# Eight input tiles accumulated side by side, k-outer, inside the modulation stage

## The chip, the cores and the metric

The kernel runs on one core of a Trainium2 chip, in one launch. The metric is the device time in microseconds. The core has TensorE (PE in the profile), whose weight loads have a row of their own (PEld), VectorE (DVE), ScalarE (ACT), GpSimd (POOL, here only an issuer of DMAs) and SyncE (SP, an issuer of DMAs). Each runs its own instruction list in order; semaphores tie them together.

## The reference, cut to what matters

Two layers of one block, then a second, different block that the change leaves alone.

```python
mod = silu(c) @ w_ada[l] + b_ada[l]
shift, scale, gate = jnp.split(mod, 3, axis=-1)
h = layernorm(x) * (1.0 + scale) + shift
p = h @ w_in[l]
u_f, z_f, cq, ckv, k_r, z_a = jnp.split(p, split_pts, axis=-1)
y_f = fourier_mix(u_f, w_fmix[l]) * silu(z_f)
q = rmsnorm(cq, q_norm[l]) @ w_q_b[l]
kv = rmsnorm(ckv, kv_norm[l]) @ w_kv_b[l]
y_a = attention(q, rope(q), kv, rope(k_r)) * silu(z_a)
y = jnp.concatenate([y_f, y_a], axis=-1) @ w_out[l]
x = layernorm(ALPHA * x + gate * y, ln_g[l], ln_b[l])
```

x has 256 tokens of 2048 channels. w_ada is 2048 x 6144 a layer, w_in 2048 x 3904. `fourier_mix` takes 8 groups of 128 channels, the real part of a two-dimensional Fourier transform over tokens and channels, and multiplies by a 128 x 128 matrix for each group.

## The kernel before, in words

Everything is float32 to full precision: each operand is cut into a high and a low part (`_hi`, `_lo`, ScalarE casts the high part, VectorE subtracts for the low one), and each product is three matmuls, `mm3` (L401): low weight by high activation, high by low, high by high.

**Weights** come as a stream of chunks of 128 x 2048 (1 MiB), loaded by SP into `raw`, which has three places. A chunk's `split` makes `w_hi` (ScalarE, L880) and `w_lo` (VectorE, L1266), each in two halves, into one of two slots. Chunk g + 2 is split once chunk g is used (`after`). `landed`, `hi_ready`, `lo_ready` and `weights_used` count along. In layer order the chunks are: seven tiles of 128 output columns (four of cq, two of ckv, one with k_r and its rotated copy), `L_DFT` (the matrix of the transform over tokens, split into `dft_hi`, `dft_lo`), `L_FMIX` (w_fmix and the channel transform), then u and z tiles alternately for eight groups, then heads and output. In one tile chunk all 16 row blocks k of the same 128 columns lie side by side, and PE makes 48 matmuls of 256 columns (`chunk`).

**Modulation.** For layer 0 shift and scale are computed first, from 32 chunks `ada0` of 1 MiB. Each is eight passes with csil (the silu of c) as a stationary operand of one column (`ada_row`, L539). The chunks have four places (three in `area`, one in `raw`); SP loads one when the chunk four before it is used. Four chunks make a row of 512 values, kept in PSUM bank 6 or 7. ScalarE copies it (`take_row`), PE turns it into columns (`turn_row`, L551), VectorE adds the bias (`read_mod0`). With two rows, a quarter of x (4 of 16 row blocks k) is normalised (`stage`), transposed by PE (`turn_tokens`, L453), scaled by ScalarE (`modulated`) and cut into `a_hi`, `a_lo` by VectorE (`split_modulated`). In layer 0 two tiles already run in quarters between the rows (`two_chunks`), from row 4 on; in layer 1 the same two run in quarters after the transposes (`first_two`).

All other modulation values (the gate of layer 0, all of layer 1 and its gate) are summed by VectorE: `add_ada` (L1283) multiplies a chunk of 128 x 2048 by one value a partition and adds it to `ada_acc`. GpSimd loads these chunks into a ring of two places, `ada_ring`, each when the add two before it is done. A layer makes 16 adds before its gate is summed by PE (`gate_sum`, L526). Seven of them stand in the seven-tile stretch, one behind each tile's split; then the groups make two each in groups 0 to 3, one in group 4, none in 5 and 6.

**After the seven tiles.** During each, ScalarE squares a tile (L951) and VectorE sums the squares for the rms norms. Then PE sums them over partitions (L590), waits for the DFT chunk, and makes the Fourier weight product: four `mm3` of 512 columns from `L_FMIX`, read by ScalarE (L962) and VectorE into `cw_hi`, `cw_lo`. Each group q is then: u tile into bank 0, `seq_dft(q-1)` into bank 2, z tile into bank 1, and the channel transform of u by `cw` into bank 3. ScalarE makes `u_hi`, `t_hi` (L988) and the tanh of z (L985), VectorE `u_lo`, `t_lo`, the gate product (`gate`) and y. `seq_dft(q)` waits for `t_lo` of group q. `latents` (L1497) makes the normalised cq and ckv out of PSUM after groups 4 and 5.

Of the kernel before, what the change touches and what calls it, by code (L numbers as in the profile page):

```python
# [21 lines left out]
ALU = mybir.AluOpType  # L22
# [3 lines left out]
P = 128  # L26
# [24 lines left out]
L_DFT = LAT  # L51
L_FMIX = LAT + 1
L_FOUR = LAT + 2
# [27 lines left out]
BLK = 512  # L81
R_GATE, R_LNG, R_LNB, R_MIX, R_MLP = 0, DEPTH, 2 * DEPTH, 3 * DEPTH, 3 * DEPTH + 1

# [25 lines left out]
def build(nc, stream, ada0, ada, vectors, rows, taps, consts, positions, x, meta, out):  # L109
    with ExitStack() as ctx:  # L110
# [93 lines left out]
        def ada0_slot(s):  # L204

            return raw[:, 2 * CH:3 * CH] if s == 3 else area[:, s * CH:(s + 1) * CH]

        def lat_ps(m):

            return bank(4 + m % 3, m // 3 * T)  # L210
# [37 lines left out]
        ada0_landed = [sem(f"ada0_landed{i}") for i in range(4)]  # L248
# [24 lines left out]
        cw_h, cw_l = sem("cw_h"), sem("cw_l")  # L273
# [35 lines left out]
        def _(sp):  # L309
            sp.dma_start(vec[:, :], vectors).then_inc(vec_in, 16)  # L310
            for s in range(4):
                sp.dma_start(ada0_slot(s), ada0[s]).then_inc(ada0_landed[s], 16)
# [6 lines left out]
            def load(g, par, waits):  # L319


                if waits:
# [7 lines left out]
            load(0, 0, False)  # L330
            load(1, 1, False)
            with sp.Fori(1, ADA0 // 4) as i:
                for s in range(4):
# [3 lines left out]
            sp.wait_ge(landed[0], 16)  # L337
            sp.wait_ge(ada0_used, ADA0)
            load(2, 0, False)
            sp.wait_ge(landed[1], 16)  # L340
            sp.wait_ge(lo_ready, 2)
            load(3, 1, False)
            with sp.Fori(2, CHUNKS // 2) as i:
# [56 lines left out]
        def _(pe):  # L400
            def mm3(o, w, a, first, last):  # L401

                pe.matmul(o, w[1], a[0], start=first, stop=False)  # L403
                pe.matmul(o, w[0], a[1], start=False, stop=False)  # L404
                return pe.matmul(o, w[0], a[0], start=False, stop=last)  # L405
# [29 lines left out]
            def turn_tokens(n, q):  # L435
# [18 lines left out]
                o.then_inc(tr_ps, 1)  # L454

# [75 lines left out]
            def ada_row(r):  # L531
                if r >= 2:
                    pe.wait_ge(row_in, r - 1)
                for s in range(4):
                    pe.wait_ge(ada0_landed[s], 16 * r + 16)
                    w = ada0_slot(s)
                    for k in range(4):
                        c = KT + 4 * s + k
                        o = pe.matmul(ps[32 * k:32 * k + 1, (6 + r % 2) * 512:(7 + r % 2) * 512], csil[:, c:c + 1],  # L539
                                      w[:, k * 512:(k + 1) * 512], start=s == 0, stop=s == 3)  # L540
                    o.then_inc(ada0_used, 1)

            def turn_row(r):
# [4 lines left out]
                if r >= 4:  # L548
                    pe.wait_ge(col_in, r // 2 - 1)
                for t in range(4):  # L550
                    o = pe.matmul(bank(2 + r // 2 % 2, 4 * (r % 2) + t, 1), row[:, t * P:(t + 1) * P],  # L551
# [5 lines left out]
            for r in range(ADA0 // 4):  # L557
                ada_row(r)
                if r:
                    turn_row(r - 1)  # L560
                if r == 1:
# [3 lines left out]
                if r == 2:  # L565
                    pe.wait_ge(ln_var, NORM["meta"] + 1)
                    turn_tokens(0, 0)
                if r in (4, 6):
                    turn_tokens(0, r // 2 - 1)
                    two_chunks(0, (lat_ps(0), lat_ps(1)), a_ops, 0, r // 2 - 2)  # L570
            turn_tokens(0, 3)
            turn_row(ADA0 // 4 - 1)
            two_chunks(0, (lat_ps(0), lat_ps(1)), a_ops, 0, 2)
            two_chunks(0, (lat_ps(0), lat_ps(1)), a_ops, 0, 3)

            for l in range(DEPTH):
                G = l * PER_LAYER

                if l:
                    first_two(G, (lat_ps(0), lat_ps(1)), a_ops, 1)  # L580
                for m in range(2, LAT - 1):
                    if m >= 3:
                        pe.wait_ge(lat_sq, 6 * l + m - 2)
                    chunk(G + m, (G + m) % 2, lat_ps(m), a_ops)
                if l:
                    pe.wait_ge(mod_ready, 3)
                chunk(G + LAT - 1, (G + LAT - 1) % 2, bank(7), a_ops)

                pe.wait_ge(lat_acc, 6 * (l + 1))
                pe.matmul(bank(3, 0, 2 * T), ones[:, :], sc[:, 0:2 * T], start=True, stop=True)\  # L590
                    .then_inc(lat_stat, 1)

                pe.wait_ge(lo_ready, 2 * (G + L_DFT) + 2)
                pe.wait_ge(weights_used, G + L_DFT)
                pe.nop().then_inc(weights_used, 1)
# [4 lines left out]
                pe.wait_ge(kr_rot, l + 1)  # L600
                for j, b in enumerate((0, 1, 2, 7)):
                    o = mm3(bank(b, 0, 512), wb(g % 2, 8 + j // 2), wb(g % 2, 4 * (j % 2), 512), True, True)
                o.then_inc(weights_used, 1)

                def seq_dft(q, first):

                    pe.wait_ge(t_l, 8 * l + q + 1)
                    if first:
                        pe.wait_ge(cw_l, 4 * l + 3)
# [9 lines left out]
                def group(q, first, second=False):  # L619
                    g = G + L_FOUR + 2 * q  # L620
                    g0 = G + L_FOUR
                    if first:
                        pe.wait_ge(cw_l, 4 * l + 1)
                    chunk(g, g0 % 2, bank(0), a_ops)
                    if first:
                        pe.wait_ge(cw_l, 4 * l + 2)
                    else:
                        seq_dft(q - 1, second)
                        pe.wait_ge(z_ready, 16 * l + q)
                    chunk(g + 1, (g0 + 1) % 2, bank(1), a_ops)  # L630
                    pe.wait_ge(u_l, 8 * l + q + 1)
                    if first:
                        pe.wait_ge(cw_l, 4 * (l + 1))
                        pe.wait_ge(ln_var, NORM[f"lat{l}"] + 1)
                    for j in range(2):
                        o = mm3(bank(3, j * T), (u_hi[:, j * P:(j + 1) * P], u_lo[:, j * P:(j + 1) * P]),
                                (cw_hi[:, bass.ds(q * T, T)], cw_lo[:, bass.ds(q * T, T)]), True, True)
                    o.then_inc(t_ps, 1)

                group(0, True)  # L640
                group(1, False, True)
                with pe.Fori(2, GROUPS - 1) as q:
                    group(q, False)
                gate_sum(l)
                group(GROUPS - 1, False)
# [6 lines left out]
                def project(h, first):  # L652

                    g = G + L_HEAD + 2 * h
                    par = (G + L_HEAD) % 2
# [1435 lines left out]
```

## Time and profile before

| what | us |
|---|---|
| median of 3 runs | 2208.07 |
| lowest, highest run | 2205.77, 2210.68 |
| profiled execution, its own time | 2209.09 |
| its span, first to last instruction | 2207.3 |
| PE busy | 2044.4 |
| weight loads busy | 1879.5 |
| VectorE busy | 1446.1 |
| ScalarE busy | 911.8 |
| granted clock of TensorE, mean share of full speed | 0.958 |

The span is that of one profiled execution, and its instruction times add up to it, not to the median. Busy shares are means over stages with different limits, so a stage has to be read by itself. In a timeline a row is start, duration, engine, line, operation, what it writes and reads, count; a bracket gives the idle time before it and what ended it. Matmuls overlap, so their distance is the cost of one, not their duration. A stored count x8 on L539 is one chunk. Times of the trace are us from the span's start.

### The profile page before, as it was taken

Reading aid. Unit: us, or ns where it says so; the run is one execution under the profiler, and the core shown is the slowest. Engines: PE = TensorE matmul, PEld = TensorE weight load, DVE = VectorE, ACT = ScalarE, POOL = GpSimd, SP = SyncE. Lnnn points to the kernel's source line nnn. Section 1 sums busy time; section 2 is a strip of 40 time slices with the busy share of each in tenths; the row PEclk is TensorE's granted clock in tenths of the full one; section 3 lists DMA queues with packets and bytes.
Section 4 is the critical chain, followed back from the end, with each engine's and each line's share of the span. In section 5 each row is a group of like instructions: output and inputs, shape, how many; then the busy total and the mean of one; then the engine's idle time right before and its main releaser. Section 6 shows DMA issues by size and latency. Waiting matters only on the chain.

```text
span 2207.3 us, 37641 instructions
## 1 busy us (share of the span) xinstructions
PE 2044.4 (93%) x14132; PEld 1879.5 (85%) x14132; DVE 1446.1 (66%) x1923; ACT 911.8 (41%) x1347; POOL 39.0 (2%) x77
## 2 busy tenths in 40 slices
PE   4889997985899999699997999989999999999998
PEld 1489997875899998599997999879989989989986
DVE  3288787798786665788898545555555545545545
ACT  2143454432344553343334334445434434434443
POOL 0000000000000000000000000000000000000000
PEclk7799998996999999899998999999999999999999
DMA  9898577593884445244453554544555555555553
GB/s 389 360 364 310 200 272 265 224 344 135 310 326 148 153 164 193 103 172 172 175 186 119 186 186 178 189 170 171 190 191 184 185 197 182 185 193 188 189 190 134
DMA packets 64192, 462.08 MB, mean 209 GB/s; under 512 B 7120, under 2 KB 7632, under 8 KB 8176
## 3 DMA queue, kind: packets, MB, share of 16 engines
q1 hardware_dynamic: 53696, 385.33, 47.4%
q0 software_dynamic: 10416, 75.63, 9.3%
q8 instruction: 57, 0.93, 0.2%
q14 instruction: 23, 0.19, 0.0%
HBM read 458.83 MB, written 2.10 MB: 209 GB/s over the span
## 4 chain that ended last, share of the span: by engine, by line
PE 78%; DVE 11%; DMA 6%; issue 3%; ACT 2%; DVEq 0%; SPq 0%; ACTq 0%; POOLq 0%
PE ps L403 25%; PE ps L404 25%; PE ps L405 25%; DVE w_lo L1266 3%; DMA raw<-in_ada 3%; DMA area<-in_ada 3%; DVE area L1288 2%; ACT w_hi L880 1%; PE ps L539 1%; DVE X L1649 0%; PE ps L453 0%; ACT sc L1036 0%; DVE X L1643 0%; DVE st L1274 0%; PE ps L516 0%
## 5 line engine op out<-in xcount | busy, mean ns | idle before, releaser
L1266 DVE TENSOR_TENSOR w_lo<-raw,w_hi 128x1024 fp32r<-128x1024 f32 x658 | 777.3, 1221 | 347.3 <-ACT w_hi L880 345.6
L403 PE MATMUL ps<-a_hi,w_lo 128*128 128x256 f32 (+1 forms) x2912 | 829.4, 285 | 16.9 <-DVE y_lo L1274 7.2
L880 ACT CAST w_hi<-raw 128x1024 fp32r (+1 forms) x658 | 656.3, 1047 | 439.7 <-PE ps L405 430.6
L404 PE MATMUL ps<-a_lo,w_hi 128*128 128x256 f32 (+1 forms) x2912 | 827.8, 284 | 0.0
L405 PE MATMUL ps<-a_hi,w_hi 128*128 128x256 f32 (+1 forms) x2912 | 826.6, 284 | 0.0
L403 PEld LDWEIGHTS ps<-a_hi,w_lo 128*128 128x128 f32 x2912 | 556.1, 191 | 20.5 <-DVE y_lo L1274 8.1
L405 PEld LDWEIGHTS ps<-a_hi,w_hi 128*128 128x128 f32 x2912 | 556.1, 191 | 0.0
L404 PEld LDWEIGHTS ps<-a_lo,w_hi 128*128 128x128 f32 x2912 | 553.1, 190 | 0.7 <-issue 0.5
L403 PE MATMUL ps<-w_hi,y_lo 128*128 128x512 f32 x768 | 300.4, 391 | 6.1 <-DVE w_lo L1266 6.1
L404 PE MATMUL ps<-w_lo,y_hi 128*128 128x512 f32 x768 | 299.4, 390 | 0.0
L405 PE MATMUL ps<-w_hi,y_hi 128*128 128x512 f32 x768 | 299.3, 390 | 0.0
L403 PEld LDWEIGHTS ps<-w_hi,y_lo 128*128 128x128 f32 x768 | 144.6, 188 | 38.1 <-DVE w_lo L1266 8.2
L405 PEld LDWEIGHTS ps<-w_hi,y_hi 128*128 128x128 f32 x768 | 144.5, 188 | 30.3
L404 PEld LDWEIGHTS ps<-w_lo,y_hi 128*128 128x128 f32 x768 | 144.6, 188 | 29.4
L1288 DVE SCALAR_TENSOR_TENSOR area<-area,csil 128x2048 f32<-128x2048 f32 x64 | 150.3, 2349 | 20.2 <-DMA area<-in_ada 17.2
L1205 ACT ACTIVATE sc<-ps 128x256 f32<-128x256 f32 x64 | 24.6, 385 | 180.6 <-PE ps L405 180.6
L1900 DVE TENSOR_TENSOR sc<-sc 128x256 f32<-128x256 f32 x64 | 27.3, 426 | 105.2 <-ACT sc L1205 105.2
L403 PE MATMUL ps<-y_hi,w_lo 128*128 128x256 f32 x272 | 78.7, 289 | 8.9 <-DVE y_lo L1816 5.8
L404 PE MATMUL ps<-y_lo,w_hi 128*128 128x256 f32 x272 | 78.4, 288 | 0.0
L405 PE MATMUL ps<-y_hi,w_hi 128*128 128x256 f32 x272 | 78.3, 288 | 0.0
L1274 DVE TENSOR_TENSOR st<-ps,st 128x256 fp32r<-128x256 f32 (+1 forms) x98 | 48.0, 505 | 20.6 <-ACT st L980 17.8
L403 PEld LDWEIGHTS ps<-y_hi,w_lo 128*128 128x128 f32 x272 | 53.6, 197 | 9.2 <-issue 6.0
(229 smaller groups left out, 1935.7 us busy)
## 6 DMA issues: line engine op xcount, KB each, us to landing
raw<-in_stream SPq DMA_DIRECT2D x331, 1024.0 KB, 4.8
area<-in_ada POOLq DMA_DIRECT2D x64, 1024.0 KB, 5.3
area<-in_ada SPq DMA_DIRECT2D x24, 1024.0 KB, 8.0
raw<-in_ada SPq DMA_DIRECT2D x8, 1024.0 KB, 9.3
grow<-in_rows POOLq DMA_DIRECT2D x4, 1024.0 KB, 5.1
area<-in_rows POOLq DMA_DIRECT2D x4, 1024.0 KB, 7.1
X<-in_x SPq DMA_DIRECT2D x1, 2048.0 KB, 15.2
out<-X SPq DMA_DIRECT2D x4, 512.0 KB, 2.6
```

The lines of the kernel that those rows point to most:

```text
L403: pe.matmul(o, w[1], a[0], start=first, stop=False)
L404: pe.matmul(o, w[0], a[1], start=False, stop=False)
L405: return pe.matmul(o, w[0], a[0], start=False, stop=last)
L539: o = pe.matmul(ps[32 * k:32 * k + 1, (6 + r % 2) * 512:(7 + r % 2) * 512], csil[:, c:c + 1], w[:, k * 512:(k + 1) * 512], start=s == 0, s ...
L880: ac.copy(to, raw[:, bass.ds((g % RAW) * CH + h * n, n)]).then_inc(hi_ready, 1)
L1205: ac.activation(sc[:, b * T:(b + 1) * T], bank(b), ACT.Relu).then_inc(f_relu, 1)
L1266: ve.tensor_tensor(to, raw[:, bass.ds((g % RAW) * CH + h * n, n)], hi.bitcast(F32), ALU.subtract).then_inc(lo_ready, 1)
L1274: return ve.tensor_tensor(out_, exact, hi.bitcast(F32), ALU.subtract)
L1288: ve.scalar_tensor_tensor(out=ada_acc, in0=ada_ring[:, par * CH:(par + 1) * CH], scalar=csil[:, bass.ds(KT + a % KT, 1)], in1=ada_acc, op0 ...
L1900: ve.tensor_tensor(s, r, r, ALU.mult).then_inc(f_sq, 1)
```

## The change

The first eight column tiles of a layer (the seven, and u of group 0) are stored in two column blocks of four tiles; a chunk now holds four row blocks k of four tiles (`by_block`), and there are eight such chunks in the order quarter, column block (`FIRST = 8`). PE works through them in `piece`s: one row block k, four tiles, 12 matmuls. All eight tiles stay open in PSUM banks 4 to 7, two tiles a bank.

In layer 0 a piece stands behind each modulation chunk from number 10 on, 22 in all, and the last ten follow. The stream's eight chunks are loaded between modulation chunks 4 and 31. The modulation chunks have three places, not four, and the row stays in one bank. In layer 1 the eight chunks run as four quarters (`quarter_of`) between the transposes.

Then the Fourier weight product comes at once (`L_FMIX` before `L_DFT`), z of group 0 into bank 2 with the norm's sum in the middle of it, and the channel transform of u. Squares and their sums are made after the eight tiles. `slot_of` gives the slot of a chunk, now that the DFT chunk uses none. Of the 16 adds of a layer, three stand ahead of group 0, two in each of groups 0 to 5 and one in group 6.

```diff
-L_DFT = LAT
-L_FMIX = LAT + 1
-L_FOUR = LAT + 2
+FIRST = 8
+L_FMIX = FIRST
+L_DFT = FIRST + 1
+L_FOUR = FIRST + 1
...
-            return bank(4 + m % 3, m // 3 * T)
+            return bank(4 + m // 2, m % 2 * T)
...
-            with sp.Fori(1, ADA0 // 4) as i:
-                for s in range(4):
-                    sp.wait_ge(ada0_used, 4 * i + s - 3)
-                    sp.dma_start(ada0_slot(s), ada0[bass.ds(4 * i + s, 1)].rearrange("a p n -> (a p) n"))\
-                        .then_inc(ada0_landed[s], 16)
...
+            for c in range(3, ADA0):
+                sp.wait_ge(ada0_used, c - 2)
+                sp.dma_start(ada0_slot(c % 3), ada0[c]).then_inc(ada0_landed[c % 3], 16)
+                if c % 8 in (4, 6):
+                    g = c // 8 * 2 + (c % 8) // 6
+                    load(g, g % 2, g >= 2)
+            with sp.Fori(FIRST // 2, CHUNKS // 2) as i:
...
+            def piece(l, q, j, kk):
+
+                g, k = l * PER_LAYER + 2 * q + j, 4 * q + kk
+                if kk % 2 == 0:
+                    half(g, kk // 2)
+                    pe.wait_ge(ln_lo, 8 * l + k // 2 + 1)
+                for m in range(4):
+                    at = j * CH + kk * BLK + m * P
+                    o = mm3(lat_ps(4 * j + m), (w_hi[:, at:at + P], w_lo[:, at:at + P]), a_ops(k),
+                            k == 0 and m % 2 == 0, k == KT - 1, True)
+                if kk == 3:
+                    o.then_inc(weights_used, 1)
...
+            for c in range(ADA0):
+                ada_chunk(c)
+                if c % 4 == 0 and c:
+                    turn_row(c // 4 - 1)
...
+                if c % 8 == 7:
+                    turn_tokens(0, c // 8)
+                if c >= 10:
+                    n = c - 10
+                    if n == 0:
+                        pe.wait_ge(ln_var, NORM["meta"] + 1)
+                    piece(0, n // 8, n % 8 // 4, n % 4)
+            piece(0, 2, 1, 2)
             turn_row(ADA0 // 4 - 1)
+            piece(0, 2, 1, 3)
+            quarter_of(0, 3)
...
+                    turn_tokens(1, 0)
+                    turn_tokens(1, 1)
+                    quarter_of(1, 0)
+                    for q in range(1, 4):
+                        if q < 3:
+                            turn_tokens(1, q + 1)
+                        quarter_of(1, q)
...
+                g = G + L_FOUR + 1
+                pe.wait_ge(cw_l, 4 * l + 2)
+                half(g, 0)
+                blocks(slot_of(g), bank(2), a_ops, range(8), True, False)
+                pe.wait_ge(lat_acc, 6 * (l + 1))
+                pe.wait_ge(cw_l, 4 * l + 4)
+                pe.matmul(bank(1, 0, 2 * T), ones[:, :], sc[:, 0:2 * T], start=True, stop=True)\
+                    .then_inc(lat_stat, 1)
+                half(g, 1)
+                blocks(slot_of(g), bank(2), a_ops, range(8, 16), False, True).then_inc(weights_used, 1)
...
@@ VectorE, a layer from its eighth tile on
-                    add_ada(A + m, (A + m) % 2)
+                lat_add(0)
+                lat_add(1)
                 cw(0)
                 cw(1)
-                after(G + L_FMIX, G + L_FMIX)
+                split(G + L_DFT, None, True)
+                split(G + L_DFT + 1, 1)
                 cw(2)
                 cw(3)
+                for m in range(2, QT + CT):
+                    lat_add(m)
+                split(G + L_DFT + 2, 0)
+                ve.wait_ge(lat_stat, l + 1)
...
                 def group(q, first, adds=2, late=False):
-                    a0 = A + (2 if late else LAT)
+                    a0 = A + 3 if not late else A + 2
...
+                    gate(q, 2 if first else 1)
+                    if first:
+                        add_ada(a, a0 % 2)
                     after_ada(g + 1, g0 + 1, a + 1, (a0 + 1) % 2, adds > 1)
                     ve.wait_ge(t_h, 8 * l + q + 1)
                     sub_hi(t_lo, bank(3, 0, 2 * T), t_hi).then_inc(t_l, 1)
 
+                for a in range(3):
+                    add_ada(A + a, a % 2)
                 group(0, True)
                 with ve.Fori(1, GROUPS // 2) as q:
                     group(q, False)
-                group(GROUPS // 2, False, 1)
+                group(GROUPS // 2, False)
                 latents(range(3))
-                group(GROUPS // 2 + 1, False, 0)
+                group(GROUPS // 2 + 1, False)
                 latents(range(3, QT + CT))
-                group(GROUPS // 2 + 2, False, 0)
+                group(GROUPS // 2 + 2, False, 1)
```

## Rows read from the trace of the kernel before

**Rows 1.** Windows: PE, PEld, DVE, ACT, POOL busy us (xcount), granted clock, DMA share, GB/s

```profile
5.00:105.40 100.40, 65.04 (x402) 24.75 (x403) 27.21 (x59) 17.97 (x30) 1.19 (x2) 0.75 0.93 381
105.40:142.90 37.50, 36.24 (x289) 36.04 (x290) 31.05 (x31) 14.59 (x22) 3.18 (x6) 0.94 1.00 394
142.90:180.90 38.00, 32.11 (x228) 30.01 (x227) 30.39 (x30) 18.76 (x24) 2.65 (x5) 0.91 0.85 321
534.30:579.90 45.60, 44.32 (x353) 44.09 (x354) 35.99 (x42) 17.01 (x28) 3.18 (x6) 0.94 0.65 242
579.90:620.30 40.40, 32.63 (x228) 30.63 (x227) 30.57 (x30) 17.46 (x23) 2.65 (x5) 0.87 0.79 303
620.30:692.20 71.90, 71.90 (x586) 69.98 (x586) 59.17 (x68) 32.08 (x50) 3.18 (x6) 1.00 0.70 255
```

**Rows 2.** Timeline of PE, modulation stage: start us, us, what, idle before

```profile
27.18 1.89 PE L539 MATMUL ps<-area,csil 128*1 128x512 f32 x8 [12.01 <-DMA area<-in_ada]
29.67 1.71 PE L539 MATMUL ps<-area,csil 128*1 128x512 f32 x8 [0.60 <-DMA area<-in_ada]
...
62.64 1.89 PE L539 MATMUL ps<-area,csil 128*1 128x512 f32 x8 [1.35 <-DMA area<-in_ada]
...
69.06 1.05 PE L551 MATMUL ps<-csil,rs 128*128 128x1 f32 x8
69.97 1.07 PE L453 MATMUL ps<-con,grow 128*128 128x128 f32 x8
...
100.52 1.04 PE L539 MATMUL ps<-raw,csil 128*1 128x512 f32 x8 [1.88 <-DMA raw<-in_ada]
...
103.84 1.70 PE L551 MATMUL ps<-csil,rs 128*128 128x1 f32 x8
```

**Rows 3.** Timeline of PE: matmuls at either clock

```profile
71.12 0.28 PE L405 MATMUL ps<-a_hi,w_hi 128*128 128x256 f32 x1
...
105.77 0.41 PE L404 MATMUL ps<-a_lo,w_hi 128*128 128x256 f32 x1
105.98 0.41 PE L405 MATMUL ps<-a_hi,w_hi 128*128 128x256 f32 x1
```

**Rows 4.** Timeline of PE, layer 1, after a wait

```profile
593.16 0.58 PE L403 MATMUL ps<-a_hi,w_lo 128*128 128x256 f32 x1 [4.45 <-DVE y_lo L1274]
```

**Rows 5.** Timeline of DVE, layer 0

```profile
107.36 0.69 DVE L1274 TENSOR_TENSOR a_lo<-grow,a_hi 128x512 fp32r<-128x512 f32 x1
...
149.13 2.35 DVE L1288 SCALAR_TENSOR_TENSOR area<-area,csil 128x2048 f32<-128x2048 f32 x1 [2.20 <-DMA area<-in_ada]
151.40 2.35 DVE L1266 TENSOR_TENSOR w_lo<-raw,w_hi 128x1024 fp32r<-128x1024 f32 x2
153.67 1.28 DVE L1274 TENSOR_TENSOR y_lo<-ps,y_hi 128x512 fp32r<-128x512 f32 x2
...
158.34 0.87 DVE L1495 TENSOR_SCALAR rs<-ps 128x256 f32<-128x256 f32 x2
...
172.68 0.68 DVE L1274 TENSOR_TENSOR st<-ps,st 128x512 fp32r<-128x512 f32 x1
```

**Rows 6.** Timeline of ACT, layer 0

```profile
126.08 0.39 ACT L951 ACTIVATE sc<-ps 128x256 f32<-128x256 f32 x1 [3.41 <-PE ps L405]
126.36 1.99 ACT L880 CAST w_hi<-raw 128x1024 fp32r<-128x1024 f32 x2
131.76 0.39 ACT L951 ACTIVATE sc<-ps 128x256 f32<-128x256 f32 x1 [3.41 <-PE ps L405]
...
151.65 1.07 ACT L962 CAST y_hi<-ps 128x512 fp32r<-128x512 f32 x2 [4.58 <-PE ps L405]
```

**Rows 7.** DMA issues, 583 to 660 us: KB each, median us to landing

```profile
area<-in_ada POOLq DMA_DIRECT2D x8, 1024.0 KB, 5.1
```

**Rows 8.** Timeline of DVE, layer 1, around the latents

```profile
665.26 3.34 DVE L1501 RECIPROCAL rs<-rs 128x512 f32<-128x512 f32 x1
...
671.36 0.42 DVE L1274 TENSOR_TENSOR st<-ps,st 128x256 fp32r<-128x256 f32 x1
```

More of the change, by code:

```diff
@@ L247, in build @@
         weights_used = sem("weights_used")
-        ada0_landed = [sem(f"ada0_landed{i}") for i in range(4)]
+        ada0_landed = [sem(f"ada0_landed{i}") for i in range(3)]
         ada0_used = sem("ada0_used")
@@ L319, in load @@
             def load(g, par, waits):
-                if waits:
+                if waits and isinstance(g, int):
+                    if g >= RAW:
+                        sp.wait_ge(lo_ready, 2 * g - 2 * RAW + 2)
+                    sp.wait_ge(landed[par], 8 * (g - par))
+                elif waits:
                     split_before = sp.snap(sp.to_reg(2 * g - 2 * RAW + 2))
@@ L400, in _, with mm3 @@
         def _(pe):
[L401 to L405, printed above, removed]
+            def mm3(o, w, a, first, last, shared=False):
+                pe.matmul(o, w[1], a[0], start=first, stop=False, skip_group_check=shared)
+                pe.matmul(o, w[0], a[1], start=False, stop=False, skip_group_check=shared)
+                return pe.matmul(o, w[0], a[0], start=False, stop=last, skip_group_check=shared)
             def wb(par, k, n=P):
@@ L454, in turn_tokens, with quarter_of @@
                 o.then_inc(tr_ps, 1)
+            def piece(l, q, j, kk):
[9 more added lines that the diff above has]
+                    o.then_inc(weights_used, 1)
+            def quarter_of(l, q):
+                for p in range(8):
+                    piece(l, q, p // 4, p % 4)
             def two_chunks(g, outs, ops, n, q):
@@ L528, in gate_sum, with ada_chunk @@
                 o.then_inc(ada_summed, 1)
[L531 to L541, printed above, removed]
+            def ada_chunk(c):
+                r, s = divmod(c, 4)
+                if r and s == 0:
+                    pe.wait_ge(row_in, r)
+                pe.wait_ge(ada0_landed[c % 3], 16 * (c // 3 + 1))
+                for k in range(4):
+                    at = KT + 4 * s + k
+                    o = pe.matmul(ps[32 * k:32 * k + 1, 2 * 512:3 * 512], csil[:, at:at + 1],
+                                  ada0_slot(c % 3)[:, k * 512:(k + 1) * 512], start=s == 0, stop=s == 3)
+                o.then_inc(ada0_used, 1)
             def turn_row(r):
@@ L617, in seq_dft, with group @@
                     o.then_inc(yf_ps, 1)
-                def group(q, first, second=False):
+                def group(q, second=False):
                     g = G + L_FOUR + 2 * q
[L621 to L633, printed above, removed]
-                        pe.wait_ge(ln_var, NORM[f"lat{l}"] + 1)
[L635 to L641, printed above, removed]
+                    g0 = slot_of(G + L_FOUR + 2)
+                    chunk(g, g0, bank(0), a_ops)
+                    seq_dft(q - 1, second)
+                    if second:
+                        pe.wait_ge(ln_var, NORM[f"lat{l}"] + 1)
+                    pe.wait_ge(z_ready, 16 * l + q)
+                    chunk(g + 1, 1 - g0, bank(1), a_ops)
+                    to_tokens(q)
+                group(1, True)
                 with pe.Fori(2, GROUPS - 1) as q:
-                    group(q, False)
+                    group(q)
                 gate_sum(l)
-                group(GROUPS - 1, False)
+                group(GROUPS - 1)
                 pe.wait_ge(lat_l, 6 * (l + 1))
@@ L1062, in _ @@
                     root("pre1b", 1, 1e-6)
-                    ac.wait_ge(mod_ready, 3)
-                    for q in range(4):
-                        modulated(1, q)
                 else:
@@ L1254, in _, with split @@
             own = Chain(ve, dve)
-            def split(g, par, dft=False, halves=range(2)):
+            def split(g, slot, dft=False, halves=range(2)):
                 n = HALF // 2 if dft else HALF
@@ L1448, in _ @@
             stage(0, 0)
+            stage(0, 1)
             for q in range(4):
+                split(2 * q, 0)
                 read_mod0(q)
@@ L1452, in _ @@
                 split_modulated(0, 2 * q + 1)
-                if q < 3:
-                    stage(0, q + 1)
-            ve.wait_ge(ada0_used, ADA0)
+                split(2 * q + 1, 1)
+                if q < 2:
+                    ve.wait_ge(ln_lo, 2 * q + 2)
+                    stage(0, q + 2)
             clear_ada(2)
@@ L1700, in _ @@
                             stage(1, q + 2)
+                        if q:
+                            for j in range(2):
+                                split(PER_LAYER + 2 * q + j, j)
                 else:
```

223 lines of the change are left out of this document (105 added, 118 removed).

## The prediction

> **What bounds the kernel now.** The page's table of 40 slices showed where PE is not full: near the start, briefly at each layer's latent stage, and at the end of each layer. Windows cut at the events the change touches [rows 1], and the timelines of PE, DVE and ACT, were read next. In the modulation stage (5 to 105.4 us) the DMA engines are 93% busy and PE's busy time contains long waits: this stage is paid by transfers. From 105.4 PE streams products with a DVE that is itself 80 to 85% busy in the seven-tile stretch. From 142.9 to 180.9 (last latent-type tile, to the end of the second z tile) and from 579.9 to 620.3 PE has idle time and a lower granted clock; afterwards it is full until 692.2. So three bounds follow one another: DMA, then PE, then for a few microseconds the chain ACT, DVE, PE around the Fourier product.
>
> **The modulation stage after the change.** Thirty-two modulation chunks and two stream chunks are loaded under it now, and eight stream chunks later: six more. Neighbouring chunks land 2.49 us apart [rows 2], so six cost 15 us of transfer, less the some 7 us in 5 to 105.4 in which DMA was not busy. The serial order by 2.49 us puts modulation chunk 10 at 42 us. That is the first with a `piece` behind it.
>
> The 48 matmuls of a tile take 5.68 us (squares at 126.08 and 131.76 [rows 6]), 0.118 each. A piece is 12 of them: 1.42 us or, at the lower clock with one every 0.21 us, 2.56 us [rows 3]. A chunk's own eight passes take 1.04 or 1.89 us (0.97 without the overlapping tail), a turned row 1.05, a turned quarter 1.07 [rows 2]. Eight chunks thus ask 8 x (0.97 + 1.42) + 1.07 + 2 x 1.05, or 22.3 us of PE at the higher clock, against 10 transfers or 24.9 us. It fits, but not evenly: no stream load comes between chunks 7 and 12, PE falls up to 3 us behind there, and with three slots, not four, that delays the next load. Following the order by hand gives 25.6 us for each eight and 113.7 us for the last landing; saturated DMA would give 109. A drop of the granted clock at the gap beside a stream load (the chunk behind a 1.35 us wait took 1.89 [rows 2]) costs 1 to 3 us more. I take 115, bounds 109 and 123.
>
> Behind the last chunk: its passes, transposes, three pieces and a turned row, 5.9 us to the row's end; 2.5 us until the first low halves (103.84 + 1.70 to 107.36 + 0.69 in the row of two [rows 2, 5]); then eight pieces, 11.4 us, and 0.7 us for a slow start: 20.5. Eight tiles are finished at Q = 135.5. Before, seven were at 142.9 and u0 needed 48 x 0.118 = 5.7 more. Up to Q, layer 0 gains 13 us.
>
> **Layer 1 up to Q.** PE starts at 534.3 as before. Eight tiles are 384 x 0.118 = 45.4 us, two quarters of transposes 2.1, the low clock at the start 2.4: Q = 584.2, against 579.9 for seven. The two weight splits a quarter need 4 us of ACT and 4.7 of DVE [rows 5, 6] beside 11.4 us of PE and are hidden. The old waits between the quarters of two tiles (a little over 1 us) go.
>
> **From Q to the second z tile.** Here the change moves work the wrong way. The seven `add_ada` that DVE made in the tile stretch, in time that it had, now stand behind the squares, splits and Fourier products: three before `group(0)`, two in it, all ahead of the `t_lo` for which PE's first `seq_dft` waits, in front of all later PE work.
>
> DVE after Q: u_lo and kr 0.5 to 1.3 us; two squares in turn with ACT (0.39 and 0.42 each) to 2.6; two Fourier low halves of 0.64 to 3.9; the DFT split 1.3 (half the columns of a 2.35 one) to 5.2; the z0 split 2.35 to 7.5; two more low halves to 8.8; four squares in turn with ACT to 11.9; the split of u1, whose ACT half is free only at 12.45, to 14.8; the sums 0.87, to 15.7 [rows 5, 6]. PE starts z0 at 6.5, waits for the squares in the middle of it, and ends u1 near 22.
>
> Then the adds, 2.35 each [rows 5]: two landed long ago, to 20.4. The ring has two places, so the third load is issued when the first add ends (18.05) and lands 5.1 us after its issue [rows 7], which comes 0.7 us behind the add (0.53 of it GpSimd's own, 3.18 us for six [rows 1]): 23.9, add to 26.2. gate 26.6. The fourth has landed, to 29.0. The fifth's load leaves at 26.2, lands 32.0, add to 34.4. Split of the next chunk 36.7, t_lo 37.3. PE has stood for 15 us, from Q+22.2. Then seq_dft 1.4, z1 5.7, and 1.6 us because matmuls after a wait run at the lower clock (0.58 us behind a 4.45 us wait [rows 4], 20 of them at 0.213 in place of 0.118): z1 ends at Q + 46.0.
>
> The Trainium skill, "DMA: Bandwidth & Descriptors", section "Anatomy of one DMA", gives a fixed 2.0 us plus bytes by 436 GB/s for a load issued by GpSimd, an estimate of 4.4 us for 1 MiB, where the row has 5.1. By the page each of the two waits would be 0.7 us shorter and z1 would end at Q + 44.6; the row decides.
>
> Layer 0: 135.5 + 46.0 = 181.5 against 180.9, +0.6. Layer 1: 584.2 + 46.0 = 630.2 against 620.3, +9.9. Bounds of the 46.0: 39.5 if no add waited for its load, 49 if the loads meet the stream's.
>
> **Groups 4 to 6.** Before, these made one add; now five, 9.4 us more, next to the latents (reciprocal 3.34, latents of three tiles until 671.36 [rows 8]). DVE in 620.3 to 692.2 is 59.17 of 71.9 us busy [rows 1], and much of the rest is waiting for ACT inside a group. Laid over the old timeline: group 4's extra add makes the split for u6 late by 2.3 us, group 5's two make t_lo late by another 2.4. Together +4.7 per layer, bounds 0 (the gaps take it all) and 8. Groups 1 to 3 keep their two adds. Heads, output and the second block keep their work. The moved PSUM banks and the weight slot indices cost nothing: same instructions, and each reader is still ahead of the next writer.
>
> **Sum.** +0.6 + 9.9 + 2 x 4.7 = +19.9 us. The profiled execution took 2209.09 us with a span of 2207.3, so 2229.0 on its scale; the median shown is 1.0 lower: 2228. A coarser check is by DVE work alone: at Q in layer 1 it owes six adds more than at 579.9 (14.1 us) and starts 4.3 us later; of its 22 idle us until 692.2 it may win back 3 to 10. That gives +8 to +15, mine is +14.6.
>
> **Rivals.** (A) The forecast, chance 0.58, own range 2217 to 2239.
>
> (B) Faster: the 13 us gained up to Q in layer 0 stand because t_lo comes in time. With PE never waiting for t_lo, z1 ends at Q + 30.9: -14.5 in layer 0, -5.2 in layer 1, and with the group losses 2198. Each us of PE's wait for the first t_lo costs 2 us (two layers); the sign turns at 5 us of wait, I have 15. For it: DVE has idle time before Q. Against: adds are in program order behind it. Chance 0.14.
>
> (C) Slower still: TensorE's granted clock falls in the modulation stage. Eight chunks then ask 41 us of PE, not 22.3. With half of them at the lower clock, 9.5 us per eight less 3.3 us of slack, over 21 chunks: +16 us, 2244. For it: 62 to 69 us ran slow with short waits. Against: when PE is behind it has no gaps. Chance 0.13. The Trainium skill, "TensorE: Matmul & The Clock Gate", section "HAM oscillation", describes this: products of a tile shorter than the wait for its next slice, so that each tile starts slow. By it every stream gap would begin slow and (C) would be the likelier; the rows show both outcomes in this stage.
>
> (D) The lower bounds together: DMA saturated (-6), group losses absorbed (-9.4), t_lo 3 us earlier in each layer (-6): 2207. Chance 0.15, of which 0.09 within the band.
>
> **Numbers.** 0.2% (4.4 us) is what a measurement of this kernel tells from no change. Slower: A, C and 0.06 of D, 0.77; same 0.09; faster 0.14. The range from 2204 to 2243 leaves out B and half of C.
>
> **What the new profile would show.** The chunks after number 10 about 3.2 us apart on average and the last matmul of the modulation near 115; two rows of pieces at 0.28, not 0.41; the first Fourier product near 136 and 584; a PE wait of 10 to 18 us ended by DVE's `t_lo` in each layer, with two DVE waits on `area<-in_ada` before it; short PE waits on `w_lo` or `t_lo` in groups 5 and 6. Wrong if this wait is under 5 us, or if pieces in the modulation stage are mostly 0.41.

## The result, and the profile after

The kernel before took 2206.96 us (median of 4 runs, 2205.77 to 2210.68), the changed one 2231.68 us (median of 4, 2226.5 to 2233.33). The ratio is 1.0105, with a 95% interval of 1.0084 to 1.0126: slower by 24.7 us. The forecast was 2228, with a range of 2204 to 2243. The profiled execution of the changed kernel is its fastest: 2226.5 us with a span of 2224.8, which is 17.5 more than the span before. All ratios are of fast runs alone: one run of experiment 1, slow at 4033 us, is left out.

**Windows of the changed kernel**, cut at the same events as those of before, with two more inside the modulation stage. The columns are those of [rows 1].

```profile
20.00:40.00 20.00, 10.60 (x50) 2.00 (x50) 8.07 (x23) 5.53 (x9) 0.00 (x0) 0.59 1.02 424
65.00:120.00 55.00, 46.99 (x368) 30.69 (x368) 15.11 (x22) 14.22 (x20) 0.00 (x0) 1.00 0.98 385
120.40:140.30 19.90, 18.77 (x157) 17.73 (x158) 8.77 (x11) 6.40 (x9) 1.72 (x3) 1.00 0.79 287
140.30:186.10 45.80, 26.86 (x178) 25.17 (x178) 32.40 (x35) 17.88 (x28) 3.16 (x6) 0.78 0.67 252
538.60:587.60 49.00, 48.97 (x401) 49.00 (x402) 25.61 (x32) 18.13 (x24) 0.53 (x1) 0.96 0.46 165
587.60:633.20 45.60, 26.77 (x178) 25.07 (x178) 32.39 (x35) 16.57 (x27) 3.17 (x6) 0.81 0.69 258
633.20:709.60 76.40, 72.75 (x590) 70.42 (x589) 67.28 (x72) 31.96 (x50) 5.28 (x10) 1.00 0.78 282
```

The gain is in the second and third lines: PE works through the pieces at full granted clock under the loads, and the eight tiles are done at 140.3. Before, the seven were done at 142.9. The loss is in the two lines of 46 us. Each of them holds the work from the eighth tile to the second z tile. PE is busy for less than 27 of 46 us, while before it was busy for 32 of 38 and 33 of 40 [rows 1].

**PE waits by releaser, changed kernel**: first from 105 to 300 us (layer 0), then from 545 to 740 us (layer 1). The columns are the total in us, the number of waits and the longest.

```profile
PE ps L408 <- DVE st L1315: 17.0, 2, 15.0
PE ps L408 <- DVE w_lo L1307: 5.1, 2, 3.4
...
PE ps L408 <- DVE st L1315: 16.9, 2, 14.9
PE ps L408 <- DVE w_lo L1307: 5.1, 2, 3.4
```

L1315 on `st` is here the low half `t_lo`. One wait of 15 us a layer stands for the first of them, and one of 2.0 us for a later one. The split `w_lo` adds 3.4 and 1.7 us.

**Timeline of PE, changed kernel, layer 0**: the transposes of the first quarter of x, a matmul of a piece, the last modulation chunk, and the two waits.

```profile
41.46 1.97 PE L458 MATMUL ps<-con,grow 128*128 128x128 f32 x8 [4.39 <-DVE grow L1385]
...
71.03 0.28 PE L410 MATMUL ps<-a_hi,w_hi 128*128 128x256 f32 x1
...
120.41 1.04 PE L562 MATMUL ps<-area,csil 128*1 128x512 f32 x8 [2.21 <-DMA area<-in_ada]
...
146.44 0.35 PE L408 MATMUL ps<-a_hi,w_lo 128*128 128x256 f32 x1 [3.42 <-DVE w_lo L1307]
...
176.88 0.58 PE L408 MATMUL ps<-st 128*128 128x256 f32 x1 [15.04 <-DVE st L1315]
```

**Timeline of DVE, changed kernel, layer 0**, while PE stands.

```profile
151.97 2.36 DVE L1307 TENSOR_TENSOR w_lo<-raw,w_hi 128x1024 fp32r<-128x1024 f32 x2 [0.51 <-ACT w_hi L908]
154.24 0.88 DVE L1541 TENSOR_SCALAR rs<-ps 128x256 f32<-128x256 f32 x2
155.03 4.81 DVE L1329 SCALAR_TENSOR_TENSOR area<-area,csil 128x2048 f32<-128x2048 f32 x2
163.54 2.35 DVE L1329 SCALAR_TENSOR_TENSOR area<-area,csil 128x2048 f32<-128x2048 f32 x1 [3.70 <-DMA area<-in_ada]
165.81 0.41 DVE L1578 SCALAR_TENSOR_TENSOR zs<-th,ps 128x256 f32<-128x256 f32 x1
166.14 2.35 DVE L1329 SCALAR_TENSOR_TENSOR area<-area,csil 128x2048 f32<-128x2048 f32 x1
171.61 2.35 DVE L1329 SCALAR_TENSOR_TENSOR area<-area,csil 128x2048 f32<-128x2048 f32 x1 [3.12 <-DMA area<-in_ada]
173.88 2.35 DVE L1307 TENSOR_TENSOR w_lo<-raw,w_hi 128x1024 fp32r<-128x1024 f32 x2
176.15 1.01 DVE L1315 TENSOR_TENSOR st<-ps,st 128x512 fp32r<-128x512 f32 x2
```

This is the forecast's chain: five adds of 2.35 us (the row x2 holds two) and two waits for a load, 3.70 and 3.12 us, all between the norm sums and the `t_lo` that releases PE. In layer 1 the same two waits are 3.24 and 3.49 us. The loads behind them, GpSimd's from 583 to 660 us, beside those of [rows 7]:

```profile
area<-in_ada POOLq DMA_DIRECT2D x10, 1024.0 KB, 5.3
```

**Timeline of DVE, the gate sum's end in each layer**: first the kernel before, then the changed one.

```profile
252.90 2.47 DVE L1314 TENSOR_TENSOR grow<-grow,ps 128x512 f32<-128x512 f32 x4
...
692.30 2.47 DVE L1314 TENSOR_TENSOR grow<-grow,ps 128x512 f32<-128x512 f32 x4
```

```profile
263.00 2.47 DVE L1355 TENSOR_TENSOR grow<-grow,ps 128x512 f32<-128x512 f32 x4
...
710.16 2.47 DVE L1355 TENSOR_TENSOR grow<-grow,ps 128x512 f32<-128x512 f32 x4
```

The first `a_lo` of layer 1 is at 533.5 before and 537.8 after. So the account of the 17.5 us of span is: layer 0 up to its gate +10.1; heads and output, up to that `a_lo`, 274.8 us against 280.6, or -5.8; layer 1 up to its gate 172.4 against 158.8, or +13.6; the rest -0.4. The change leaves the code of that stretch alone, and other kernels with the same code there take 276.5 to 278.9 us (last section), so at least a part of the -5.8 is chance of this one execution. Without it the sum is +23.3, near the 24.7 of the medians.

### The profile page after: what moved, and what is told of

It is laid out like the page before. It is cut to its first block, busy times and chain, and to the rows that moved or that the text cites. A ratio compares the mean times of both kernels' runs of the same rounds, so it can differ in the third digit from the quotient of the medians.

```text
span 2224.8 us, 37536 instructions
## 1 busy us (share of the span) xinstructions
PE 2035.9 (92%) x14132; PEld 1875.1 (84%) x14132; DVE 1445.0 (65%) x1923; ACT 911.7 (41%) x1347; POOL 38.9 (2%) x77
## 4 chain that ended last, share of the span: by engine, by line
PE 76%; DVE 13%; DMA 5%; issue 3%; ACT 2%; DVEq 0%; ACTq 0%; POOLq 0%; SPq 0%
PE ps L408 24%; PE ps L409 24%; PE ps L410 24%; DMA area<-in_ada 5%; DVE w_lo L1307 4%; DVE area L1329 2%; PE ps L562 1%; ACT w_hi L908 1%; DVE st L1315 1%; PE ps L458 1%; DVE X L1699 0%; DVE y_lo L1315 0%; ACT sc L1080 0%; DVE X L1693 0%; PE ps L539 0%
## 5 line engine op out<-in xcount | busy, mean ns | idle before, releaser
L408 PEld LDWEIGHTS ps<-a_hi,w_lo 128*128 128x128 f32 x2912 | 555.3, 191 | 36.2 <-issue 27.7
L408 PE MATMUL ps<-st 128*128 128x256 f32 x160 | 47.8, 299 | 40.3 <-DVE st L1315 40.3
L562 PE MATMUL ps<-area,csil 128*1 128x512 f32 x256 | 38.8, 686 | 33.9 <-DMA area<-in_ada 33.2
```

The costliest lines, as they stand in the source:

```text
L408: pe.matmul(o, w[1], a[0], start=first, stop=False, skip_group_check=shared)
L562: o = pe.matmul(ps[32 * k:32 * k + 1, 2 * 512:3 * 512], csil[:, at:at + 1], ada0_slot(c % 3)[:, k * 512:(k + 1) * 512], start=s == 0, stop ...
```

## The experiments

The theory going in: DVE's adds, moved behind the eighth tile, cost the time, and the loads of a ring of two places lengthen them. Its rivals: other parts of the new order, or a modulation stage in which PE is late. Ratios are to the kernel before, run beside the changed one on the same chip. Medians of different experiments come from different chips, so they compare less well than ratios.

**1. Both adds of group 0 behind `t_lo`.**

```diff
+                    after_ada(g + 1, g0 + 1, a + 1, (a0 + 1) % 2, adds > 1 and not first)
+                    ve.wait_ge(t_h, 8 * l + q + 1)
+                    sub_hi(t_lo, bank(3, 0, 2 * T), t_hi).then_inc(t_l, 1)
                     if first:
                         add_ada(a, a0 % 2)
-                    after_ada(g + 1, g0 + 1, a + 1, (a0 + 1) % 2, adds > 1)
-                    ve.wait_ge(t_h, 8 * l + q + 1)
-                    sub_hi(t_lo, bank(3, 0, 2 * T), t_hi).then_inc(t_l, 1)
+                        add_ada(a + 1, (a0 + 1) % 2)
```

> Changed kernel, with the two adds of group 0 behind t_lo instead of ahead of it. Adds theory: t_lo of group 0 ends 7 to 8 us earlier in each layer (two adds of 2.35 us and one wait of 3.1 to 3.5 us for a load), PE's wait of 15.0 us for it falls to about 7.5, and the time from 2231.7 to about 2217. Rival (the new order around the Fourier product, with its squares and splits, sets the wait, and the adds only fill it): the wait stays at 13 to 15 us and the time within 3 us of 2231.7.

Measured: 2228.02 us, ratio 1.0107 (1.0084 to 1.0131), no change that the times can tell, where about 2217 was expected. The PE waits of layer 0 (105 to 300 us) in this kernel:

```profile
PE ps L408 <- DVE st L1315: 11.1, 3, 6.9
PE ps L408 <- DVE w_lo L1307: 6.4, 3, 3.4
```

The first wait fell from 15.0 to 6.9 us as expected, but others came back behind it, and the gate was only 3.1 us earlier in either layer. The forecast of this run took the wait for the cost. What costs is what DVE owes: two adds and their loads, put behind one `t_lo`, delay the next one.

**2. The five adds ahead of the first `t_lo` on 16 of their 2048 columns.** The rest of these terms is left out of the modulation sums.

```diff
-            def add_ada(a, par):
+            def add_ada(a, par, n=CH):
...
-                    add_ada(A + a, a % 2)
+                    add_ada(A + a, a % 2, 16)
```

> Changed kernel; the five adds of each layer that stand ahead of the first t_lo take only 16 of their 2048 columns (the other columns of these five terms are left out), semaphores and loads as before. It parts DVE's time in them from the waits for their loads. Adds theory: 11 us of DVE time go, but the loads still come two at a time with about 5.8 us from add to landing, so t_lo ends 6 to 7 us earlier in each layer and two waits on area<-in_ada are longer than before; time near 2218. Were the waits for loads nothing, it would be 11 us a layer and 2210. Rival (adds only fill a wait that others set): no change of the wait for t_lo, 2231.

Measured, in a single run: 2218.94 us beside 2203.86 for the kernel before, so 15.1 more than it, against 24.7 for the whole change. The gate of layer 0 comes 5.0 us earlier than in the changed kernel, and layer 1 is 4.7 us shorter up to its gate. The timeline of DVE in layer 0:

```profile
162.17 0.23 DVE L1329 SCALAR_TENSOR_TENSOR area<-area,csil 128x16 f32<-128x16 f32 x1 [6.79 <-DMA area<-in_ada]
165.60 0.24 DVE L1329 SCALAR_TENSOR_TENSOR area<-area,csil 128x16 f32<-128x16 f32 x1 [2.87 <-DMA area<-in_ada]
168.08 0.23 DVE L1329 SCALAR_TENSOR_TENSOR area<-area,csil 128x16 f32<-128x16 f32 x1 [2.24 <-DMA area<-in_ada]
170.50 1.01 DVE L1315 TENSOR_TENSOR st<-ps,st 128x512 fp32r<-128x512 f32 x2
```

With the arithmetic nearly gone, `t_lo` comes 5.6 us earlier, not 11: the loads of the ring set the pace instead. PE's wait is still 9.6 us.

**3. One product in place of three in the 22 pieces of layer 0's modulation stage.** The two low products of these pieces are left out.

```diff
-                    piece(0, n // 8, n % 8 // 4, n % 4)
+                    piece(0, n // 8, n % 8 // 4, n % 4, True)
```

> Changed kernel; the 22 pieces between the modulation chunks make one product in place of three (low parts left out, only there). It asks why the last modulation chunk came at 120.4 us and not at the 109 of an unbroken DMA. Theory (with three places PE's lateness delays the next load): the last chunk's passes begin at 109 to 112 us, and the time is 8 to 10 us less, near 2222. Rival (the transfers themselves are slower than 2.49 us each): they begin at 118 or later and the time falls by less than 3 us.

Measured, in a single run: 2231.42 us, and the last chunk's passes begin at 120.19 (120.41 in the changed kernel). So it is not PE's products that delay the last landing. This kernel's windows:

```profile
40.00:65.00 25.00, 19.81 (x100) 8.63 (x100) 12.34 (x20) 7.58 (x11) 0.00 (x0) 0.93 0.78 314
65.00:120.00 55.00, 38.88 (x240) 18.35 (x240) 14.93 (x22) 14.19 (x20) 0.00 (x0) 0.82 0.98 396
```

With a third of the product work the DMA engines still idle a fifth of 40 to 65 us and then move 396 GB/s. The idle part lies in one place. The changed kernel, and then that of experiment 7:

```profile
40.00:46.00 6.00, 4.54 (x28) 2.75 (x32) 4.63 (x10) 1.32 (x2) 0.00 (x0) 0.63 0.34 109
46.00:65.00 19.00, 14.65 (x116) 8.89 (x108) 7.83 (x12) 6.41 (x9) 0.00 (x0) 1.00 0.99 404
...
40.00:46.00 6.00, 6.00 (x31) 2.41 (x33) 2.39 (x6) 1.55 (x4) 0.00 (x0) 0.50 0.71 247
```

Behind modulation chunk 7 PE waits 4.39 us for DVE to normalise the first quarter of x (the 41.46 row above). The next chunk is used only afterwards, so no place comes free, SP's queue waits up to 7.5 us for these passes, and the DMA engines run dry: 34% busy in 40 to 46 us, 99% from there to 65. With one product this wait is 4.40 us and the share 25%. So PE does hold the loads back once, by a wait and not by its work.

**4. The kernel before, with nothing but the adds' new places**: `add_ada` taken out of the seven-tile stretch, three ahead of group 0, two in each of groups 0 to 5 and one in group 6.

```diff
-                    add_ada(A + m, (A + m) % 2)
...
+                for a in range(3):
+                    add_ada(A + a, a % 2)
```

> The kernel before, tiles and Fourier product as they were; only VectorE's adds are placed as in the changed kernel: none in the seven tiles, three ahead of group 0, two in groups 0 to 5, one in group 6. Adds theory: t_lo of group 0 comes 6 to 8 us too late for PE, groups 4 to 6 lose 4 to 5 us, in each layer: 2207 becomes 2227 to 2233. Rival (the adds cost nothing where they stand, the tiles' new order costs): within 4 us of 2207.

Measured: a median of 2223.95 us, 20.1 more than the kernel before (2203.86), the low end of the 20 to 26 that were expected; the ratio is 1.0105 (1.0066 to 1.0143), that of the whole change. One of the four runs took 2237.17 us, 13 more than the next, and widens the interval; the two medians alone make 1.0091. The PE waits of layer 0:

```profile
PE ps L403 <- DVE w_lo L1266: 7.5, 4, 2.8
PE ps L403 <- DVE st L1274: 6.1, 2, 4.1
```

No single wait here is longer than 4.1 us, yet the gate of layer 0 comes 7.7 us later than before (260.61), and layer 1 takes 8.4 us more from its first `a_lo` to its gate (707.87 less 540.65, against 158.8). Moved alone, in the old order of everything else, the adds cost two thirds of the change's 23.7 us by stage (10.1 and 13.6) and by the ratio as much as all of it, with an interval from 15 to 32 us. So most of the loss needs no other part of the change.

**5. In layer 1, six adds in the quarters, one ahead of group 0**, then 2, 2, 2, 2, 1, 0, 0 in the groups. GpSimd loads four chunks more ahead of the gate row.

```diff
+                                add_ada(5 * KT + 2 * (q - 1) + j, j)
...
-                for a in range(3):
+                for a in (range(6, 7) if l else range(3)):
...
-                group(GROUPS // 2, False)
+                group(GROUPS // 2, False, 1 if l else 2)
```

> Changed kernel; in layer 1 alone six adds stand behind the weight splits of quarters 1 to 3, one ahead of group 0, and the groups have 2, 2, 2, 2, 1, 0 and 0 as in the kernel before; GpSimd loads four of these chunks ahead of the gate's row. Debt theory (it is DVE's total of adds behind the eighth tile that counts, not where they stand in it): six adds are paid in idle time, PE's wait for the first t_lo of layer 1 falls from 15 us to about 4, the waits of groups 5 and 6 of layer 1 go; 15 us less than the changed kernel, ratio to the kernel before near 1.004. Rival (the Fourier part sets the wait): less than 4 us off, ratio 1.009 or more.

Measured: ratio 1.0062 (1.0047 to 1.0078), clearly below the changed kernel's but short of the 1.004 expected. Layer 1 from its first `a_lo` to its gate takes 160.3 us, 12.1 less than 172.4, where 15 was expected. PE's wait for the first `t_lo` fell to 6.4 us, not to 4, and the waits of groups 5 and 6 are gone. One of the two load waits is left:

```profile
617.04 2.35 DVE L1333 SCALAR_TENSOR_TENSOR area<-area,csil 128x2048 f32<-128x2048 f32 x1 [2.80 <-DMA area<-in_ada]
```

**6. Four of a layer's adds in groups 4 to 6 on 16 columns**, the rest of these terms left out.

```diff
...
-                group(GROUPS // 2 + 1, False)
+                group(GROUPS // 2 + 1, False, n=(16, 16))
...
```

> Changed kernel; the second add of group 4 and those of groups 5 and 6 (four a layer) take only 16 of 2048 columns (the rest of these terms is left out). Theory: PE's waits of groups 5 and 6 go, 4 to 5 us a layer, 8 to 10 us in all: ratio to the kernel before near 1.0065. Rival (these adds stand in gaps, the forecast's lower bound): within 2 us of the changed kernel, ratio 1.010.

Measured: the two later waits are gone, and the stages are 4.8 us (layer 0) and 4.4 us (layer 1) shorter, as the forecast's +4.7 a layer asks. The ratio, 1.0094 (1.0078 to 1.0109), moved by only 0.0011, less than its interval can tell; the expected 1.0065 lies outside the interval, the rival's 1.010 inside. In the profiled execution the span is only 3.8 us shorter, though the two stages are 9.2 us shorter: the stretch between layer 0's gate and layer 1 took 3.7 us more. So the profile bears out the two waits and their price by stage, and the times do not show that the whole kernel gains them.

**7. The stream's loads spread evenly over the modulation stage**, one behind every fourth chunk, the eighth behind the last.

```diff
-                if c % 8 in (4, 6):
-                    g = c // 8 * 2 + (c % 8) // 6
+                if c % 4 == 0:
+                    g = c // 4 - 1
                     load(g, g % 2, g >= 2)
+            load(7, 1, True)
```

> Changed kernel; the stream loads of the modulation stage come one behind every fourth modulation chunk (4, 8, ... 28) and the eighth behind the last, in place of two close together in each eight. Theory of the order (PE falls behind in the long stretch without stream load): the last modulation chunk's passes begin 3 to 5 us earlier, near 116, and the kernel is as much faster: ratio near 1.009. Rival, which the run with one product speaks for (transfers run at some 385 GB/s in this stage whatever PE does): only the one transfer moved behind the last chunk shows, 2.5 us, ratio 1.0095 or more.

Measured: ratio 1.0082 (1.0063 to 1.0101). The last chunk's passes begin at 114.09, 6.3 us earlier, and the gate of layer 0 comes 6.9 us earlier. Windows of this kernel:

```profile
40.00:65.00 25.00, 24.58 (x171) 13.60 (x169) 9.62 (x14) 7.00 (x10) 0.00 (x0) 0.85 0.91 360
65.00:120.00 55.00, 48.56 (x387) 33.02 (x384) 15.35 (x24) 14.23 (x20) 1.19 (x2) 1.00 0.98 399
```

The DMA engines are 91% busy in 40 to 65 us, where the changed kernel has 83%, and move 360 GB/s against 334. The order of the loads is worth about 6 us of layer 0, and it is a cost of its own beside the adds. An estimate of its parts: 2.5 us is the one stream load that now follows the last chunk, and 2.0 us the DMA idle time that the hole at 40 to 46 us no longer has (17% of 25 us less 9%); the rest is the higher rate behind it. It is not the long stretch without a stream load that is mended, as the theory had it: one stream load instead of two now stands ahead of chunk 7, so PE's wait for x ends at 38.56 us and not at 41.46, while the DMA engines still have the other one to move. The ratio alone does not part theory and rival: 1.009 and 1.0095 both lie inside its interval.

**8. All of it**: the edits of 5 and 7; in layer 0 the first two adds behind the split of the last modulated quarter and one ahead of group 0; in both layers the second add of group 0 behind `t_lo`. Then **9, the same without the edit of 7**.

```diff
-            clear_ada(2)
+            add_ada(ADA0, 0)
+            add_ada(ADA0 + 1, 1)
...
-                for a in range(3):
+                for a in (range(6, 7) if l else range(2, 3)):
```

> Changed kernel with layer 1's adds early (as in e3), the loads spread (as in e6), and in layer 0: ada_acc cleared as soon as the last modulation chunk is used, adds 0 and 1 behind the split of chunk 7, one add ahead of group 0, and in both layers the second add of group 0 behind t_lo. Debt theory: 15 us from layer 1, about 9 from layer 0 (two adds and both waits for loads leave the path to t_lo), 2.5 to 4 from the loads: ratio to the kernel before 0.996 to 1.000. Rival (the order of adds is worth little): ratio above 1.004.

> The kernel of e7_all without its spreading of the loads: the changed kernel with the adds of both layers placed as in e7_all, the stream's loads in the changed kernel's order. If the two costs are separate, as e6_loads_spread put them (the loads' order 6.3 us of layer 0's last modulation chunk, the adds the rest), the last chunk's passes begin at 120 us, not 114, and the time lies 6 to 7 us above e7_all's, 2203 where the kernel before has 2206, a ratio of 0.998 to 1.000. If the early loads are what lets the adds come early in layer 0, the waits for the first t_lo come back in part there as well and the time is 2207 or more, a ratio above 1.000.

Measured for all of it: 2196.35 us, ratio 0.9957 (0.9943 to 0.9970), better than both kernels. Without the spread loads: 2203.21 us, ratio 0.9989 (0.9976 to 1.0002), no longer to be told from the kernel before; the last chunk's passes begin at 121.53, and no wait for `t_lo` is longer than 2.0 us. The PE waits of the first of the two, in layer 0 and then in layer 1:

```profile
PE ps L413 <- DVE st L1320: 6.0, 4, 2.0
PE ps L413 <- DVE w_lo L1312: 5.1, 2, 3.4
...
PE ps L413 <- DVE w_lo L1312: 3.4, 1, 3.4
PE ps L413 <- DVE st L1320: 3.0, 2, 1.7
```

The gate sums of the two kernels, first of all of it, then of 9:

```profile
242.46 2.47 DVE L1360 TENSOR_TENSOR grow<-grow,ps 128x512 f32<-128x512 f32 x4
...
679.00 2.47 DVE L1360 TENSOR_TENSOR grow<-grow,ps 128x512 f32<-128x512 f32 x4
```

```profile
251.54 2.47 DVE L1359 TENSOR_TENSOR grow<-grow,ps 128x512 f32<-128x512 f32 x4
...
685.00 2.47 DVE L1359 TENSOR_TENSOR grow<-grow,ps 128x512 f32<-128x512 f32 x4
```

Against the changed kernel, 9 gains 11.5 us up to layer 0's gate (263.00 less 251.54) and 17.3 in layer 1: its first `a_lo` is at 529.90, so 155.1 us against 172.4. That sum, 28.8 us, stands beside the 28.5 between the two medians (2231.68 and 2203.21); the two ratios, 1.0105 and 0.9989, make it 25.6. The spread loads bring the next 6.9 us. So the adds' places account for about the whole loss: with them mended, the change's other parts are worth about nothing with the old order of loads, and 0.4% faster than before with the new one.

## Why the prediction was right

**The mechanism (A) held at each step in which it could be seen.**

- *Last modulation chunk.* Forecast 115, bounds 109 and 123; measured 120.4. This term was mis-sized by 5.4 us. The pieces fit as forecast: PE keeps its 0.28 us rows. But each eight chunks take 27.3 and 27.7 us (65.40, 92.72, 120.41), not the 25.6 of the hand-made order, which used 2.49 us a transfer [rows 2]. And by that order, counted back from 113.7 in steps of 25.6, chunk 15 is due at 62.5; it came at 65.40. Part of these 2.9 us is a wait that the forecast does not name: PE's 4.39 us for the first normalised quarter of x, under which the DMA engines run dry (experiment 3). Experiment 3 also rules out the reason that the forecast gave for PE falling behind, its products: with a third of them the chunk comes at 120.2.
- *From there to the eighth tile*: forecast 20.5, measured 19.9. Layer 1: forecast 49.9 us from its start, measured 49.0.
- *From the eighth tile to the end of `t_lo`*: forecast 37.3, measured 36.6 and 36.5 to PE's release. PE's wait: forecast 15 us, measured 15.04 and 14.9. The two load waits, forecast 3.5 and 3.0, measured 3.70 and 3.12 in layer 0, 3.24 and 3.49 in layer 1. The load row of [rows 7] held (5.3 us here, median of ten); by the Trainium skill, "DMA: Bandwidth & Descriptors", section "Anatomy of one DMA", both waits would have been 0.7 us shorter than forecast; the measured ones are longer.
- *To the second z tile*: forecast 46.0, measured 45.8 and 45.7. The z tile's tanh is at 186.10 (before 180.91) and 633.26 (before 620.31).
- *Groups 4 to 6*: forecast +4.7 a layer, measured +4.9 in each (z tile to gate, 76.9 us against 72.0), with exactly the two waits that the forecast laid over the old timeline, one on the split and one on `t_lo`.
- *Sums*: layer 0 forecast +5.3, measured +10.1, all the difference being the late last chunk; layer 1 forecast +14.6, measured +13.6.

**Rival B** (`t_lo` in time, 2198) needed a wait under 5 us; it was 15. Its price was sound, though. Where the wait is gone (experiment 8), z1 ends 31.5 us after the eighth tile, for the forecast's 30.9, and the time is 2196, though that kernel mends the groups and the order of the loads as well. **Rival C** (the clock falls in the modulation stage, 2244) did not come: the granted clock is 1.00 from 65 to 120 us, the higher level, with PE 85% busy (46.99 of 55.00 us) and waits of up to 2.2 us between. The forecast named the page "TensorE: Matmul & The Clock Gate", section "HAM oscillation", for it. The page's case is one of products that are shorter than the wait for their next slice; here a piece and a chunk's passes together take 2.4 us and no wait is longer than 2.23, so the forecast's reading, that by the page each such gap would begin slow, went further than the page's case. In these 55 us the trace shows no slow start. **Rival D** fell on all three counts: the last chunk came later than forecast, the groups lost all of their 4.7, and `t_lo` was 0.7 us early, not 3.

One reading of the forecast the runs corrected. It wrote "Each us of PE's wait for the first t_lo costs 2 us". Experiment 1 took 8 us off each of these waits; each gate came 3.1 us earlier, and the ratio was 1.0107. The wait showed the debt; it was not the debt.

## What to carry to other kernels

When a milestone is pulled forward, list what another engine did in its slack before it: work that then lands behind the milestone can be on the path nearly in full, with its loads. Moving such work past one release only hands the wait to the next; to win, it must go back to where the engine idles, here between the quarters. And the order in which two streams of loads share few buffers has a price of its own, to be worked out separately from what the loads feed. Whether a ring of more than two places would have done as well as moving the adds was not tried.

## What the runs showed that was not expected

**Transfers ran slower in the stage with two interleaved streams.** The changed kernel moves 424 GB/s in 20 to 40 us, where five of the six loads that it issues are modulation chunks, and 385 in 65 to 120 us, where the engines are busy for 98% of the time. In the latter stretch another order of the same loads gives 399 GB/s (experiment 7), and fewer products 396 (experiment 3). The drop is not even: the changed kernel moves 423 GB/s in 83 to 92 us, where SP issues modulation chunks alone, and 301 in 101 to 108 us, where it issues two stream loads. Why a busy queue moves less there stays open; it was not tried with loads alone.

**A stretch that the change leaves alone varied by up to 7 us between kernels**: from layer 0's gate to the first `a_lo` of layer 1 it took 280.6 us before, 274.8 in the changed kernel, and 278.0, 276.5, 278.9, 280.0, 280.8, 278.5, 278.1, 281.8 and 278.4 in experiments 1 to 9. Experiments 1, 2, 3, 6 and 7 have the changed kernel's code in this stretch, so 274.8 is short by some 3 us even among its like. In its part from 415 to 532 us DVE waits for loads of `area` 2.1 us in the changed kernel and 5.6 in experiment 5, for `in_rows` 1.8 and 4.2. These are single executions, so phase of the loads and chance are not told apart. It may be why the profiled execution, at 2226.5, is 5 us under its other three runs, of which no trace was kept: a span's difference should be read stage by stage before it is held against the forecast.

**The printed clock can disagree with the rows.** From 20 to 40 us the changed kernel and experiment 3 do the same work and the same 50 matmuls; the printed clock is 0.59 in the one and 1.00 in the other. But a chunk's passes take 1.89 us in both, their length at the lower level (1.04 us is that at the higher one). First the window and a row of experiment 3, then the changed kernel's row:

```profile
20.00:40.00 20.00, 11.77 (x50) 2.81 (x50) 8.07 (x23) 5.67 (x9) 0.00 (x0) 1.00 1.02 423
20.12 1.89 PE L566 MATMUL ps<-area,csil 128*1 128x512 f32 x8 [6.70 <-DMA area<-in_ada]
...
20.27 1.89 PE L562 MATMUL ps<-area,csil 128*1 128x512 f32 x8 [7.54 <-DMA area<-in_ada]
```

So the clock of a window is to be read together with the lengths of its rows. With loads as the bound it cost nothing here: both kernels moved the same bytes, 424 and 423 GB/s.
